# Four pairs of adaptive-modulation units moved from TensorE's column strips to VectorE, and a later begin of the strips

## The reference, cut to what matters

```python
h = rms_norm(x, mix_norm_g[l])
p = h @ w_in[l]                       # the mixers' input product
(lru_x, lru_z, ml_u, ml_o, ml_z, ml_i, ml_f,
 mo_q, mo_k, mo_v, mo_z) = jnp.split(p, SPLIT_POINTS, axis=-1)
...
# second block, i = 0 and 1; the same with c_ctx for the context
shift, scale, gate = jnp.split(jax.nn.silu(c) @ ada_w[i] + ada_b[i], 3, axis=-1)
h_lat = rms_norm_2(x, pre_norm[i]) * (1 + scale[:, None]) + shift[:, None]
```

## Time and profile before

| | |
|---|---|
| three runs | 1687.86, 1690.05, 1691.64 us; median 1690.05 |
| the profiled execution | 1690.44 us, span 1688.6 us |
| TensorE busy, mean granted clock | 1664.5 us (99%), 0.997 |
| VectorE busy | 1312.2 us (78%) |
| ScalarE busy | 763.5 us (45%) |
| loads and stores | 315.28 MB, mean 187 GB/s |
| a unit of 512 KB, from issue to landing | 4.4 us in the median |

### The profile page before, as it was taken

One profiled execution on the slowest core, in us unless ns is written; L12 is line 12 of the kernel. 1 busy time (PEld: TensorE's weight loads), 2 busy tenths in 40 slices (PEclk: granted clock), 3 DMA queues, 4 the chain that ended last, 5 costly groups with the idle time before them and its releaser, 6 DMA issues.

```text
span 1688.6 us, 26892 instructions
## 1 busy us (share of the span) xinstructions
PE 1664.5 (99%) x10702; PEld 1482.6 (88%) x10702; DVE 1312.2 (78%) x2150; ACT 763.5 (45%) x1184; POOL 30.4 (2%) x46
## 2 busy tenths in 40 slices
PE   9999999999999999999999999999989999999998
PEld 9999998988899898888888888889989899999886
DVE  7899778577657798787887779874887787888654
ACT  7533375724446653322342233323655455445443
POOL 0000000000000000000000000000000111000000
PEclk9999999999999999999999999999999999999999
DMA  8787765646686544345554556654354664444354
GB/s 294 241 285 263 240 219 182 215 153 213 234 308 231 200 139 139 135 165 172 186 184 161 182 184 221 208 183 136 126 169 161 190 193 151 131 128 135 99 177 135
DMA packets 163508, 315.28 MB, mean 187 GB/s; under 512 B 14508, under 2 KB 22840, under 8 KB 163128
## 3 DMA queue, kind: packets, MB, share of 16 engines
q1 hardware_dynamic: 152352, 288.92, 51.9%
q0 software_dynamic: 5312, 18.88, 3.9%
q10 hardware_dynamic: 5720, 5.78, 1.1%
HBM read 311.44 MB, written 2.10 MB: 186 GB/s over the span
## 4 chain that ended last, share of the span: by engine, by line
PE 70%; DVE 4%; ACT 1%; issue 1%; DMA 0%; DVEq 0%; SPq 0%; ACTq 0%
PE bank L650 17%; PE bank L651 16%; PE bank L652 16%; PE bank L3093 2%; PE bank L2676 1%; PE bank L3370 1%; PE bank L3372 1%; PE bank L3371 1%; PE bank L735 1%; PE bank L737 1%; PE bank L736 1%; PE bank L557 1%; DVE ada_acc L521 1%; PE bank L3082 1%; DVE w_low L376 1%; PE bank L2679 1%
## 5 line engine op out<-in xcount | busy, mean ns | idle before, releaser
L650 PE MATMUL bank<-operand,w_high 128*128 128x256 f32 (+2 forms) x2368 | 754.6, 319 | 10.1 <-DVE w_low L376 5.0
L651 PE MATMUL bank<-operand,w_high 128*128 128x256 f32 (+2 forms) x2368 | 744.0, 314 | 0.0
L652 PE MATMUL bank<-operand,w_low 128*128 128x256 f32 (+2 forms) x2368 | 744.0, 314 | 0.0
L366 ACT ACTIVATE w_high<-raw 128x1024 fp32r<-128x1024 f32 (+3 forms) x404 | 394.1, 1004 | 401.0 <-PE bank L652 175.7
L376 DVE TENSOR_TENSOR w_low<-raw,w_high 128x1024 fp32r<-128x1024 f32 (+3 forms) x404 | 452.5, 1156 | 85.1 <-ACT w_high L366 82.9
L650 PEld LDWEIGHTS bank<-operand,w_high 128*128 128x128 f32 x2368 | 452.2, 191 | 49.8 <-issue 10.6
L651 PEld LDWEIGHTS bank<-operand,w_high 128*128 128x128 f32 x2368 | 452.4, 191 | 28.1 <-issue 0.7
L652 PEld LDWEIGHTS bank<-operand,w_low 128*128 128x128 f32 x2368 | 452.2, 191 | 27.1
L521 DVE SCALAR_TENSOR_TENSOR ada_acc<-ada_raw,silu_c,ada_acc 128x512 f32<-128x512 f32 x464 | 318.7, 745 | 6.2 <-DMA ada_raw<-in_ada_w 3.9
L650 PE MATMUL bank<-operand_small,w_high 128*128 128x512 f32 (+1 forms) x240 | 88.3, 368 | 0.0
L651 PE MATMUL bank<-operand_small,w_high 128*128 128x512 f32 (+1 forms) x240 | 86.7, 361 | 0.0
(11 more groups left out here) (443 smaller groups left out, 1921.5 us busy)
## 6 DMA issues: line engine op xcount, KB each, us to landing
ada_raw<-in_ada_w SPq DMA_DIRECT2D x160, 512.0 KB, 4.4
raw<-in_w_in SPq DMA_DIRECT2D x96, 512.0 KB, 5.0
raw<-in_pool_w_in SPq DMA_DIRECT2D x64, 512.0 KB, 5.2
raw<-in_mla_w_in SPq DMA_DIRECT2D x48, 512.0 KB, 4.5
raw<-in_w_out SPq DMA_DIRECT2D x32, 512.0 KB, 6.5
raw<-in_pool_w_out SPq DMA_DIRECT2D x32, 512.0 KB, 5.9
ada_raw<-in_ada_w POOLq DMA_DIRECT2D x32, 512.0 KB, 4.2
raw<-in_mla_w_out SPq DMA_DIRECT2D x32, 512.0 KB, 4.7
```

The lines of the kernel that those rows point to most:

```text
L366: ins = nc.scalar.activation(view(HI[:, slot, ks, :], False), view(RAW[:, slot, ks, :], True), ACT.Copy)
L650: pe.matmul(out_, hi, x[:, 0, :], start=first, stop=False, skip_group_check=True)
L651: pe.matmul(out_, hi, x[:, 1, :], start=False, stop=False, skip_group_check=True)
L652: return pe.matmul(out_, lo, x[:, 0, :], start=False, stop=last, skip_group_check=True)
```

## The change

Units 24 to 31, eight of them, become VectorE's: two in each of chunks 12, 13, 14 and 15 of `win_c`. A sum by `pe_ada` behind chunk 15 closes them. The strips begin with unit 32 in chunk 17 and go with every chunk from 17 to 23 (seven pairs, where four of the twelve pairs of `win_c` stood in these chunks); chunks 1 to 15 have no strip any more. Chunk (1, 0) of `mixa` gets a pair. In all there are 22 pairs in place of 26. `dve_strip_columns` moves from the end of the stage ahead to the end of chunk 16.

```diff
-    SPARSE = {win_c: {divmod(c, 4): 2 for c in range(1, 24, 2)},
-              mixa: {key: 2 for key in ((0, 0), (0, 1), (1, 1), (2, 0), (2, 1), (3, 1))},
+    SPARSE = {win_c: {divmod(c, 4): 2 for c in [12, 13, 14, 15] + list(range(17, 24))},
+              mixa: {key: 2 for key in ((0, 0), (0, 1), (1, 0), (1, 1), (2, 0), (2, 1), (3, 1))},
...
-    STRIP0, STRIP1, FIRST_ROWS = 24, 76, 64
+    STRIP0, STRIP1, FIRST_ROWS = 32, 76, 64
...
             dve_evac(dve, win_b, 0)
-            dve_strip_columns(dve)
...
                 dve_beside(dve, c)
                 dve_ada(dve, win_c, i, j)
+                if c == 16:
+                    dve_strip_columns(dve)
```

## The result

The changed kernel takes 1698.26 us in the median of five executions (1697.05 to 1700.71), beside 1691.64 us for the kernel before in the five executions beside them. The ratio is 1.0047, with a 95% interval of 1.0033 to 1.0061. The profiled execution of after took 1698.16 us, 7.7 more than the profiled one of before (1690.44); the forecast was a delay of 6.3.

A forecast was written before the change was run, and what follows sets the result against it. TensorE, busy for 99% of the span, was taken to bind; -4.7 + 5.5 + 0.8 + 1.9 + 0.6 + 2.2 = +6.3 us gave a median of 1696.3 us, 0.37% slower, with a range of 1692 to 1700.7.

The forecast's parts named there:

- the clock's term: Behind the wait at the sum after chunk 15, the granted clock falls to half: +2.2 us, between nothing and 3.0.
- the 0.8 at chunk 17: TensorE waits at chunk 17 for VectorE's low half, late behind the strip columns in chunk 16: +0.8 us.
- The early chunks: Chunks 0 to 11: six pairs, 6.5 us, leave TensorE and 4.7 us of gain arrives; bounds 3.2 and 6.5.
- The wait at the sum: Behind chunk 15 TensorE idles 6.7 us for VectorE's unit 31, so chunk 16 begins 5.5 us later.
- the whole mechanism is a race from 313.07: From the gates' release, VectorE's 39.5 us of work to unit 31 runs against TensorE's reaching the sum at 345.8.
- the rival's condition: VectorE's work to unit 31 fits TensorE's 32.7 us if 6.8 us shorter; then no wait, 1686.4 us; chance 0.08.
- The bound of 3.0: Upper end of the loss from the clock's fall behind the sum, in us; the forecast took 2.2.
- Chunks 18 to 23: Three more pairs (3.2 us) and 0.5 of waiting, less 1.8 of waits at chunks 22 and 23: +1.9 us.
- The output product: In its first half one pair more, 1.08 us, and half of a strip's 1.04 us load wait goes: +0.6.
- Late loads: Rival: from chunk 17 on strips wait for their units' loads, three or four times 1.04 us, giving 1700; chance 0.13.
- The faster case: Rival: the units lie in VectorE's waits, no wait at the sum, 3.7 us gained, 1686.4 us; chance 0.08.

The follow-up runs named there:

- run with short units: Changed kernel with units 24 to 31 each working on 64 of their 512 columns: 1693.55 us, ratio to before 1.0014.
- run with three units ahead: Changed kernel with three of the eight units in win_b, two each in chunks 12 and 13, one in 14: 1689.08 us, ratio 0.9993.
- run with chunk 15 twice: Changed kernel with TensorE doing the matmuls of chunk 15 twice (48 more, 5.8 us): 1696.12 us, ratio 1.0037.
- the one that was kept busy: The best version plus 20 zero-weight matmuls (1.08 us) behind the matmuls of chunk 11: 1690.74 us, ratio 1.0005.
- the best version: Changed kernel with units in win_b and chunks 11 to 13, sum behind chunk 14, strip columns in chunk 15: 1688.57 us, ratio 0.9988.
- the small matmuls: Changed kernel with 80 zero-weight matmuls of 32 columns between chunk 15 and the sum: 1696.69 us, ratio 1.0039.

## Why the prediction was right, and where it was not

The direction and the place were right, and the size was near, in part by luck. The sum of terms came out 1.4 us short against the profiled execution: the stretch with the clock's term was 3.0 short, and smaller errors went the other way. By stretches, from the starts of the chunks in both timelines of TensorE:

| stretch | forecast | found |
|---|---|---|
| up to chunk 12 | -4.7 | -4.25 (312.86 to 308.61; at 200 us a delay of 0.32 stood, so -4.57 from there) |
| chunk 12 to 17, with the clock | +5.5 + 0.8 + 2.2 = +8.5 | +11.5 (-4.25 to 367.96 - 360.75 = +7.21) |
| chunk 17 to 23 | +1.9 | +1.6 (to 413.51 - 404.68 = +8.83) |
| output product's first half, up to its chunk 3 | +0.6 | -0.2 (to 447.48 - 438.81 = +8.67) |
| the rest | 0 | -0.9 (to the spans' 1696.4 - 1688.6 = +7.8) |

In the second row errors of both signs stand: the clock behind the sum took 5.3 for 2.2, and a second slow stretch at chunk 12 took 1.5 that was not counted; the wait was 0.7 shorter, and the 0.8 at chunk 17 did not come. So the clock, counted at 2.2, cost 6.8 in all, more than the wait of 5.96 itself.

The last row is the clock too. The delay is 8.6 us up to TensorE's wait before 1248.86 and 7.7 from 1252 on (times of before). The slow stretch behind this wait was 6.83 us long in the profiled execution of before and 3.41 in that of after, in work that the change doesn't touch:

```profile
1247.49:1254.32 6.83, 5.46 (x25) 5.46 (x26) 6.76 (x9) 3.00 (x4) 0.00 (x0) 0.50 0.32 96
1258.68:1262.10 3.42, 3.42 (x19) 3.42 (x18) 3.39 (x4) 1.06 (x1) 0.00 (x0) 0.50 0.38 101
```

*The early chunks.* Right: six pairs, 6.5 us, arrive as 4.6 from 200 us on, and TensorE's wait of 1.42 at chunk 6 is there unchanged (262.48 in after), which is the chain that swallows the rest.

*The wait at the sum.* The number was right (6.7 forecast, 5.96 found), and so were both sums behind it: VectorE took 348.80 - 308.81 = 40.0 us from the gates to unit 31 (39.5), the eight units 4.77 + 5.31 + 5.30 + 5.31 = 20.7 (20.7). The failed step is the reason that was given: "the whole mechanism is a race from 313.07", and with it the rival's condition, that VectorE's work up to unit 31 must shrink by 6.8 us. The run with short units took some 14 us out of that work and still waited 2.21. The run with three units ahead can't tell the reasons apart, as its units fit both ways. The race starts anew at each set of scores, and what counts is only what stands between the last scores and unit 31. That the sum over the whole stretch gave the right number was luck: the waits of VectorE were almost exactly as long as the six units ahead of chunk 15, so that hardly any time was left unused before it.

*The clock.* The mis-sized term. Forecast +2.2, for one slow stretch of the length of the earlier trace rows. Found: 13.65 us at 0.50, the first 1.5 of them still in the wait:

```profile
347.32:360.97 13.65, 12.12 (x48) 9.96 (x49) 8.42 (x21) 0.29 (x1) 0.00 (x0) 0.50 0.48 155
```

Lost were 0.4 us in the sum (349.86 - 348.85 = 1.0 to the next work, where 0.6 was counted), 3.0 in the work beside chunk 15 (6.7 in place of 3.7) and 20 x 0.093 = 1.9 in chunk 16, 5.3 in all. The run with chunk 15 twice gave 4.4 us back at chunk 17, and 0.78 of waiting stood in it. The bound of 3.0 was too low because it took the stretch's length from one row, behind which chunk matmuls came: that stretch is 6.83 us long in the trace of before, this one twice as long.

The Trainium skill, "TensorE: Matmul & The Clock Gate", section "HAM oscillation — how this bites in real kernels", would price 13.65 us at half of it, an estimate of 6.8. Its warning against waits in TensorE's stream is borne out here. The rows give 5.3, as 1.5 us of the stretch lay in the wait and the work beside the chunk took less than twice its time.

A second stretch was not foreseen. The windows of after around chunk 12:

```profile
304.00:309.78 5.78, 5.78 (x44) 5.13 (x44) 3.97 (x10) 5.43 (x13) 0.00 (x0) 1.00 0.02 7
309.78:313.19 3.41, 3.41 (x19) 3.41 (x18) 3.34 (x10) 3.24 (x7) 0.00 (x0) 0.50 0.02 5
```

Here 15 matmuls ran at 0.21 in place of 0.12, and chunk 12 took 1.5 us longer than at the full clock. TensorE wasn't idle ahead of it; it did the matmuls of the gates, which in the kernel before stood behind a strip pair. The same stretch of 3.4 us is there in the profiled executions of all runs with the early strips gone, save the one with short units (whose program is the same up to there) and the one that was kept busy. Why it stays away in the first of these is open; the mean clocks of that run's eleven executions go from 0.993 to 0.996, so how many slow stretches there are differs from execution to execution of one program.

*Chunk 17.* Forecast: TensorE waits 0.8 for the low half behind the strip columns. Found: no wait, since TensorE itself was late by the clock; in the runs whose clock held, it was there: 0.78 in the one with three units ahead and 0.78 with chunk 15 twice. The step was right and covered by the other's error.

*Chunks 18 to 23.* Right: 1.6 for 1.9; TensorE's waits from 361 to 421 us are one of 0.39 (2.1 and 1.0 before):

```profile
PE bank L650 <- DVE w_low L376: 0.4, 1, 0.4
```

*The output product.* Its pair of 1.08 came, and the strip's wait of 1.04 for its load went altogether; half of it had been counted.

*The rivals.* Late loads: no strip waited for one in after, with seven pairs in consecutive chunks (two other runs had one such wait each, of 0.22 and 0.34 us). The faster case was wrong in this kernel and right as a mechanism: units cost nothing where they stand ahead of a wait of VectorE. Its 1686.4 was still too good: the best version is 2.3 us faster than before, where 3.7 were counted, with 1.1 of waiting at chunk 18 and the slow stretch at chunk 12 in it.

## What to carry to other kernels

Free time of an engine is a list of waits with places: fill each up to its length, and put the last piece of work, the one that another engine is stopped for, ahead of a wait and not behind the step that ends it. For TensorE price a wait by what comes behind it as well: in the profiles here the slow stretch was 3.4 to 6.8 us behind waits of about 4 us with a chunk's large matmuls next, and 10.2 to 13.7 behind waits of 2.2 to 6.0 us with small ones next. And read the granted clock of several executions before a few us are put down to one cause, since slow stretches come and go between executions of one program. Put a sum that nobody needs yet at a place where its input is long done.

## What the runs showed of the hardware

How long the clock stayed at 0.50 did not follow the length of the wait: 10.24 us behind a wait of 2.21 with the sum, values and scores next, 3.4 us behind one of 4.01 with a chunk next. Nor is it fixed by the program: behind the wait of 3.9 us near 1250 us, with the same matmuls next in all ten kernels, it was 6.83 us in six profiles and 3.41 in four. In after the clock also fell at 309.78 with no wait of TensorE in front; the row ahead of it is of matmuls with 4 rows of the array's 128, from the timeline of TensorE:

```profile
308.09 0.59 PE L1334 MATMUL bank<-scratch 4*128 4x256 f32 x2
308.61 0.39 PE L650 MATMUL bank<-operand,w_high 128*128 128x256 f32 x1
```

And in the profiled execution 4.3 us of matmuls on 32 columns did not keep the clock up through a wait of 1.48 us and the work behind it, where 5.8 us of a chunk's matmuls did, with a wait of 0.19 left. Which of the two, the kind of matmul or the shorter wait, made that difference isn't told apart by these runs, and by its mean clock of 0.998 another execution with the small matmuls seems to have kept the clock. Nor do the runs tell where a fall of 3.4 us comes: waits of 0.78 to 1.10 us at chunks 17 and 18 had one at or right behind them in two runs and none in four others.
